# Moving one of ten per-head weight blocks into the plain stage, and the attention steps into the middle of blocks

## What is computed

```python
h = _rmsnorm(x, norm_g[l])
proj = jnp.einsum('bsd,df->bsf', h, w_in[l])
aq, ak, av, az = parts[0:4]            # branch A: 8 heads, differential attention
oa = _diff_attention(aq, ak, av, lam, slopes_a)
ya = rmsnorm(oa) * (1 - lam_init) * jax.nn.silu(az)
# branch B: three groups of q, k, v (dilations 1, 4, 16), mixed by their softmax sums
yb = ob.reshape(bsz, seq, B_WIDTH) * jax.nn.silu(bz)
# branch C: gated convolution of three taps
yc = cb * conv * jax.nn.silu(cz)
merged = sum over branches of gates[:, :, n] * (y_n @ w_branch_n)
x = x + merged @ w_out;  out = _rmsnorm(x, final_g)
```

## Time and profile before

| | |
|---|---|
| median of 3 runs | 2505.21 us (2503.38 to 2506.18) |
| the profiled execution | 2505.15 us, of which the traced span is 2503.4 us |
| PE busy | 2484.4 us, 99% of the span |
| DVE, ACT busy | 1945.7 us (78%), 1069.8 us (43%) |
| granted PE clock, mean | 0.999 of full speed |

### The profile page before, as it was taken

One profiled execution on the slowest core, in us unless ns is written; L12 is line 12 of the kernel. 1 busy time (PEld: TensorE's weight loads), 2 busy tenths in 40 slices (PEclk: granted clock), 3 DMA queues, 4 the chain that ended last, 5 costly groups with the idle time before them and its releaser, 6 DMA issues.

```text
span 2503.4 us, 30481 instructions
## 1 busy us (share of the span) xinstructions
PE 2484.4 (99%) x11454; PEld 2053.7 (82%) x11454; DVE 1945.7 (78%) x2266; ACT 1069.8 (43%) x1329; POOL 0.2 (0%) x4
## 2 busy tenths in 40 slices
PE   9999999999999999999999999999999999999998
PEld 8888888888888888888887788888878888788887
DVE  8797788566676767767678887788878888898875
ACT  5343333334333333333434433344444445655644
POOL 0000000000000000000000000000000000000000
PEclk9999999999999999999999999999999999999999
DMA  8255444686776667766535545445565456787666
GB/s 317 95 198 188 150 133 143 203 301 214 252 266 231 223 213 248 264 234 225 191 106 193 203 168 193 170 154 193 181 218 203 160 197 219 261 286 247 226 227 202
DMA packets 184902, 519.15 MB, mean 207 GB/s; under 512 B 14129, under 2 KB 59442, under 8 KB 181042
## 3 DMA queue, kind: packets, MB, share of 16 engines
q1 hardware_dynamic: 87872, 342.62, 39.9%
q10 hardware_dynamic: 96882, 174.55, 19.8%
HBM read 420.64 MB, written 96.47 MB: 207 GB/s over the span
## 4 chain that ended last, share of the span: by engine, by line
PE 92%; DVE 3%; DMA 3%; ACT 1%; issue 1%; DVEq 0%; ACTq 0%
PE proj L621 13%; PE proj L623 13%; PE proj L622 13%; PE sc_ps L621 6%; PE sc_ps L622 6%; PE sc_ps L623 6%; PE tr_ps L621 6%; PE tr_ps L622 6%; PE tr_ps L623 6%; PE o_ps L622 4%; PE o_ps L623 4%; PE o_ps L621 4%; PE tr_ps L664 1%; DVE w_lo L1547 1%; DMA rows<-c_dram 1%; DMA raw<-s_dram 1%
## 5 line engine op out<-in xcount | busy, mean ns | idle before, releaser
L1008 ACT ACTIVATE w_hi<-raw 128x1024 fp32r<-128x1024 f32 x296 | 314.0, 1061 | 430.3 <-PE proj L623 138.1
L1008 ACT ACTIVATE w_hi<-kb 128x1024 fp32r<-128x1024 f32 x280 | 297.2, 1062 | 442.6 <-PE proj L623 156.9
L1547 DVE TENSOR_TENSOR w_lo<-raw,w_hi 128x1024 fp32r<-128x1024 f32 x296 | 361.2, 1223 | 156.2 <-ACT w_hi L1008 155.3
L1547 DVE TENSOR_TENSOR w_lo<-kb,w_hi 128x1024 fp32r<-128x1024 f32 x280 | 342.7, 1224 | 116.6 <-ACT w_hi L1008 116.0
L621 PE MATMUL proj<-act_hi,w_hi 128*128 128x512 f32 x1024 | 405.8, 396 | 1.7 <-DVE w_lo L1591 1.7
L623 PE MATMUL proj<-act_hi,w_lo 128*128 128x512 f32 x1024 | 399.6, 390 | 0.0
L622 PE MATMUL proj<-act_lo,w_hi 128*128 128x512 f32 x1024 | 398.7, 389 | 0.0
L1057 ACT ACTIVATE w_hi<-raw 128x1024 fp32r<-128x1024 f32 x128 | 135.6, 1060 | 344.8 <-PE proj L623 339.9
L1591 DVE TENSOR_TENSOR w_lo<-raw,w_hi 128x1024 fp32r<-128x1024 f32 x128 | 156.6, 1224 | 103.1 <-ACT w_hi L1057 102.6
L623 PEld LDWEIGHTS proj<-act_hi,w_lo 128*128 128x128 f32 x1024 | 192.2, 188 | 41.3
L621 PEld LDWEIGHTS proj<-act_hi,w_hi 128*128 128x128 f32 x1024 | 192.8, 188 | 40.2 <-DVE w_lo L1591 1.9
(11 more groups left out here) (310 smaller groups left out, 4765.1 us busy)
## 6 DMA issues: line engine op xcount, KB each, us to landing
raw<-wg SPq DMA_DIRECT2D x128, 512.0 KB, 3.9
raw<-wst SPq DMA_DIRECT2D x128, 512.0 KB, 4.9
kb<-wg SPq DMA_DIRECT2D x28, 2048.0 KB, 7.6
ssum<-ws ACTq DMA_DIRECT2D x24, 2048.0 KB, 9.3
s_dram<-ssum ACTq DMA_DIRECT2D x24, 2048.0 KB, 7.7
raw<-s_dram SPq DMA_DIRECT2D x96, 512.0 KB, 4.4
raw<-ws SPq DMA_DIRECT2D x72, 512.0 KB, 4.1
kb<-wg SPq DMA_DIRECT2D x56, 512.0 KB, 6.3
```

The lines of the kernel that those rows point to most:

```text
L1008: nc.scalar.activation(w_hi[r % RING][:, :], src, ACT.Copy).then_inc(hi_done, 1)
L1547: tt(w_lo[r % RING][:, :], src, w_hi[r % RING][:, :].bitcast(f32), ALU.subtract).then_inc(lo_done, 1)
```

## The change

The numbering of the units changes: 9 entries and 14 units a head, and 7 quads before the branch C quads where there were 6. AZ is the plain group at the start, with weights as the stationary operand, so that the result is already transposed; it is stored to `z_dram`, comes back by head (`load_z`) and is scaled by DVE (`scale_z`). AV is quad 3. In the heads, steps stand between a block's two multiplications. (Of the diff, the parts that the steps below need.)

```diff
-NBLK1, NHU1 = 10, 16
+NBLK1, NHU1 = 9, 14
-QUADS_V, QUADS_C, QUADS_G, QUADS_O = 6, 10, 16, 2
+QUADS_V, QUADS_C, QUADS_G, QUADS_O = 7, 11, 17, 2
-SUMS_FIRST = (0, 4, 8, 12)
-SUMS_LOOP = (2, 6, 12, 16, 20, 24, 28, 34, 40, 44)
+SUMS_QUAD, SUM_QUAD_AT = 9, (13, 14, 15, 16)
+SUMS_FIRST = (0, 4, 8)
+SUMS_LOOP = (0, 4, 8, 12, 16, 20, 24, 28, 32, 36)
...
# plain_quad (PE)
-                            end = three(plain[half][b][:, :], act_hi[:, k, ts], act_lo[:, k, ts], w_hi[slot][:, cs], w_lo[slot][:, cs],
+                            end = three(plain[half][b][:, :], w_hi[slot][:, ws], w_lo[slot][:, ws], act_hi[:, k, :], act_lo[:, k, :],
...
# blocks (PE), between the two multiplications of a block
-                    if last and w == 9:
-                        values_a(i)
-                        probs_b(i, 0)
-                        scores_b(i, 1)
+                    if 4 <= w < 8:
+                        scores_a(i, w - 4)
+                    if w == BZ:
+                        scores_b(i, 0)
+                    if 5 <= w < 9:
+                        probs_a(i, w - 5)
+                    if w == 4 and not fresh:
+                        probs_b(i - 1, 3)
                     pe.wait_ge(lo_done, NHU1 * i + (R_H + t + 2))
                     multiply(h.bank(w), h.slot(t + 1), act_hi, act_lo, 8, False, True)
                     if w < 4 and not fresh:
                         scores_b(i - 1, w)
-                    if w < 5 and not fresh:
+                    if w < 4 and not fresh:
                         probs_b(i - 1, w - 1)
...
-                    if w == 5 and not fresh:
-                        values_b(i - 1)
-                    if 4 <= w < 8:
-                        scores_a(i, w - 4)
-                    if 5 <= w < 9:
-                        probs_a(i, w - 5)
-                    if w == 8:
-                        scores_b(i, 0)
...
+                    if w == 4 and not fresh:
+                        values_b(i - 1, o_ps, (o_free, 2 * i))
+                    if w == BZ:
+                        values_a(i)
+                        scores_b(i, 1)
+                        probs_b(i, 0)
...
# the first branch C quad (PE)
-                return {ON_X: [pb[2], pb[1]], ON_Z: sc_ps, ON_Y: pairs[2]}[CHAIN[p]]
+                return {ON_X: [pb[2], pb[1]], ON_Z: pairs[2], ON_Y: sc_ps}[CHAIN[p]]
-                            scores_b(HEADS - 1, 3)
+                        if n in (1, 3):
+                            scores_b(HEADS - 1, (n + 3) // 2)
-                            values_b(HEADS - 1)
+                            values_b(HEADS - 1, sc_ps[0], (biased, 8 * HEADS + 1))
...
# head (ACT)
+                    if 5 <= w < 9:
+                        turned_a(i, w - 5)
+                    if w == 4 and not fresh:
+                        turned_b(i - 1, 3)
+                    if 4 <= w < 8:
+                        exps_a(i, w - 4)
+                    if w == BZ:
+                        exps_b(i, 0)
                     split(t + 1)
...
+                        load_z(i)
...
-                    if w == AZ:
+                    if w == 7:
                         tanh_half(i, AZ)
...
# head (DVE)
+                    split(t)
...
+                    if 4 <= w < 8:
+                        bias_a(i, w - 4, fresh)
+                    if w == BZ:
+                        bias_b(i, 0)
                     if 5 <= w < 9:
-                        norm_a(i, w - 5)
-                    if w == 9:
-                        norm_b(i, 0)
-                    split(t)
+                        turned_a(i, w - 5)
+                    if w == 4 and not fresh:
+                        turned_b(i - 1, 3)
                     if w == Q0:
                         low_turn(h, AQ)
                     if w == K0:
                         low_turn(h, AK)
+                        if not fresh:
+                            inverse_a(i - 1)
+                            norm_o(i - 1)
                     if last:
                         combine_h(w)
                     if w == 4 and not fresh:
                         low_v(2 * i, v_b)
-                        inverse_a(i - 1)
-                        norm_o(i - 1)
...
-                    if w == 8:
+                    if w == BZ:
                         low_v(2 * i + 1, v_a)
-                    if w == 9:
                         silu(i, 0, AZ)
+                        norm_b(i, 0)
+                    if 4 <= w < 8:
+                        norm_a(i, w - 4)
                     scale_block(h, w)
+                    if w == 7:
+                        scale_z(i)
                     split(t + 1)
```

More of the change, by code:

```diff
@@ L702, in probs_b, with values_b @@
                 turn(i, TURN_P[c] + 1, [pr[:, n * P:(n + 1) * P] for n in range(4, 6)])
-            def values_b(i):
+            def values_b(i, bank, free):
                 pe.wait_ge(t_free, len(TURN_SPLIT) * i + (1 + len(TURN_SPLIT)))
@@ L855, in free_g @@
                     return tg_free, [len(TURN_COPY) * HEADS + 1] * 2
-                if CHAIN[p] == ON_X:
+                if q == QUADS_V + 1 and p == P5:
+                    back = (QUADS_V, 5)
+                elif CHAIN[p] == ON_X:
                     back = (q - 1, 5) if p == 0 else (q, {2: 0, 4: 2, 6: 4}[p])
@@ L1143, in squares_o @@
                 nc.scalar.activation(sq_hi[:, :], o_ps[:, :], ACT.Square).then_inc(sq_ready, 1)
+                if last:
+                    nc.scalar.activation(o_a[:, :], o_ps[:, :], ACT.Copy).then_inc(o_free, 1)
             def root_o(i, bank):
@@ L1177, in head @@
                         comb_high(6, t2[0], f2, (comb_sum, 6))
-                    if last and w == 9:
-                        squares_o(i)
-                        turned_b(i, 0)
+                    if 5 <= w < 9:
[6 more added lines that the diff above has]
+                        exps_b(i, 0)
                     split(t + 1)
@@ L1201, in head @@
                             load_v(i, Q_V + g, v_g[g], vg_in, True)
-                    if w < 5 and not fresh:
+                    if w < 4 and not fresh:
                         turned_b(i - 1, w - 1)
-                    if 5 <= w < 9:
-                        turned_a(i, w - 5)
-                    if w == 9 and not last:
+                    if w == BZ:
                         turned_b(i, 0)
@@ L1705, in scale_block, with scale_z, bias_a @@
                 ins.then_inc(evac_done, 1)
-            def bias_a(i, q):
+            def scale_z(i):
+                dve.wait_ge(za_in, 16 * i + 16)
+                tt(z_a[:, :], z_a[:, :], rstd[:, :], ALU.mult).then_inc(z_scaled, 1)
+            def bias_a(i, q, fresh):
                 n = P * (q + 1)
                 dve.wait_ge(s_ready, 8 * i + (q + 1))
-                if q:
+                if q or not fresh:
                     dve.wait_ge(p_ready, 8 * i + q)
-                else:
+                if q == 0:
                     dve.wait_ge(mask_a_in, 16 * i + 16)
@@ L1853, in head @@
                         bias_b(i - 1, w)
-                    if 4 <= w < 8:
-                        bias_a(i, w - 4)
-                    if w == 8:
-                        bias_b(i, 0)
-                    if w < 5 and not fresh:
+                    if w < 4 and not fresh:
                         turned_b(i - 1, w - 1)
-                    if 5 <= w < 9:
-                        turned_a(i, w - 5)
                     if w == 3:
@@ L2045, in _ @@
                         if n == 5:
+                            bias_b(HEADS - 1, 3)
                             turned_b(HEADS - 1, 2)
```

158 lines of the change are left out of this document (84 added, 74 removed).

## The result

The changed kernel takes 2560.38 us (median of 4, 2559.31 to 2561.66) where the kernel before takes 2504.3 us on the same chip: a ratio of 1.0224, 95% interval 1.0206 to 1.0242, or 56 us slower. The forecast was 2541, with a range up to 2560.

What follows compares the result with a forecast made beforehand. The prediction took TensorE (PE, busy 99%) to bound every stage. Waits of 46.9 us less 10.9 us for 48 fewer matmuls gave +36 us on 2505.2, so 2541, with a range of 2517 to 2560.

Steps and rivals of the forecast that it cites:

- Q1 of heads 1, 3, 4, 6: Block Q1: PE waits 5.1 us a head for `norm_b` and the bias, behind additions and reciprocal on DVE; 20 us.
- K2: Block BZ, heads 0, 1, 3, 4, 6: `scores_b(0)` waits for K2's `scale_block`, 0.9 us each, 4.5 in all.
- heads 2 and 5 together: Waits per head: 0.3 us for part 3 in Q1, 1.2 in Q0, 2 before `values_b`, 4 in BZ.
- head 7: `combine_h`, 2.3 us, stands in Q1: a wait of 2.6 us; another combination in BZ: 1.5 us.
- the quad: First branch C quad: part 3 one step later, reciprocal still before unit 7's low part; 1.9 us more (0 to 3).
- the last quad before the heads: Additions there make PE wait 1 us (0 to 3).
- 94 + 6: Expected length in us of a head of k = 1, where it was 105.
- no row here shows such a fall in the middle: Granted clock: rows showed a fall only near the end, so the waits were summed without any clock loss.
- rival 1: Heads: six waits (four in Q1, two in BZ) halve the clock, 2.5 us each, 15 us, 2556; chance 0.14.
- That queues absorb all (2): Faster: Q1's four waits vanish if the chain ends before PE's request, other waits under 1 us; 2496, chance 0.10.
- "About even" (3): Half of the Q1 waits and the smaller ones hidden, 11 us lost, 2505; chance 0.03.
- "removes nothing" (4): The count of matmuls stays, so the change does not remove what it says; chance 0.01.

Runs made afterwards that it cites:

- experiment 1: Changed kernel with spare matmuls put where PE waits in heads 1 to 7: 2544.54 us, 1.017.
- Experiment 5: Changed kernel with heads 1 to 6 written out instead of a loop, on PE, ACT and DVE: 2556.16 us, 1.0209.
- experiments 6: Changed kernel with branch B's part 3 put back by half a block in block Q1, ACT and DVE reordered to match: 2525.32 us, 1.0081.
- experiment 8: Changed kernel without the heads' additions (three one-column copies in their place, loads and stores kept): 2509.33 us, 1.0023.
- Experiments 7: Changed kernel with part 3 put back by half a block and, in BZ of heads 2 and 5, the additions behind `scale_block`: 2514.15 us, 1.0037.
- experiment 11: The order of experiment 7, with the first branch C quad's reciprocal six units later and heads 1 to 6 written out: 2506.13 us, 1.0007.
- experiment 10: The order of experiment 7, with Q0 and K2 additions behind `scale_block`, the quad's reciprocal six units later and the loop written out: 2555.14 us, 1.0202.

## Why the prediction was right and wrong

**The gain.** Right: 48 matmuls, 76.5 us for the new quad where 76.2 were worked out, 87.1 less in the heads.

**The waits.** Right in place, and nearly in sum: the terms were 46.9 us, what was measured of them, net of what was there before, is 40.2. Term by term, forecast against measured: Q1 of heads 1, 3, 4, 6 20.4 against 4 x 4.84 = 19.4; K2 4.5 against 5 x 0.43 = 2.1; heads 2 and 5 together 15 against 14.9 (`root_o` 1.2, part 3 0.6, `values_b` 3.7, `values_a` 9.3); head 7 2.6 and 1.5 against 2.5 and 0.15; the quad 1.9 against 0.95; the last quad before the heads 1 against 0.2. The large terms of Q1 and BZ came within 16%; the small ones (K2, `root_o`, the quad, BZ of head 7) were half of what was forecast, or less. A head of k = 1 took 102.2 us (AQ turned at 649.0 in head 1, at 751.2 in head 2) where "94 + 6" was forecast; its one fall of the clock took 2.1 of them.

**What failed** is the step "no row here shows such a fall in the middle", by which the sum took the clock at nothing and left it to rival 1, at 0.14 and 15 us. In its place stands a loss of 16 us by experiment 1, 19 us by the windows of the falls. The row for it was there, and the waits that I had forecast were as long as the stretch that ended in that fall. The two reasons against were both weak: the six small matmuls between the two waits in Q1 did not hold the clock up, and DVE's time to catch up was worth little, since the slow stretch reaches beyond the wait into full work. Rival 1 had the mechanism and nearly the size, with six falls of about 5 us where there were nine of 3.4 or 6.8; its 2556 came nearest to the 2560.4 measured.

**What was missing** is the jump of the loop: 4.90 us where 1.71 had been, 3.2 us. Experiment 5 shows that it goes when the loop is written out. Why it grew stays open: before, the profile puts it down to a low part, after to issue, and no run here separates the two.

With the estimated 3.9 us that the view of waits leaves out, 40.2 + 3.2 + 3.9 + 18.9 - 10.9 = 55.3 us, against 54.3 between the spans: each term is read or worked out by itself, and the sum closes within 1 us.

**The rivals.** That queues absorb all (2) fell: 28% of idle time on DVE did not help, because the chain's distance was the limit. Its condition was the right one though, the chain ending before PE's request: experiments 6 and 8 nearly meet it from either side and are at 2525 and 2509. "About even" (3) and "removes nothing" (4) fell with the first page.

**Left open.** Experiments 7 and 11 are some 4 us slower than their waits and falls account for (the eleventh: waits from 20 us on of 17.4 against 8.4, one fall worth 1.7, less 10.9, would make 2503.2 of span, and it is 2507.1). The trace places more than half of it: from 20 us on 28 waits are listed where the kernel before has 13, at 0.16 us each 2.4 us more. It shows head by head, from one turn of AQ to the next: 105.37 us in a head of the loop before, so 94.49 with two units less; with listed waits and falls taken off it is 94.7 to 95.2 us in experiment 11 and 94.5 to 94.6 in experiment 8, which has few waits. The rest, 1 to 2 us, is within what single executions differ by. Branch AV as a quad and AZ plain were not tried apart from the new order, so it is not shown that the new order was needed for them.

## What to carry to other kernels

When PE is the bound, a change that shortens a stage shortens the distance between every step and its use: redo the chain of each step in its new distance, and read which engine's queue a moved step now stands in front of, ACT's DMA issues and stores above all. Price a wait of PE of some 2 us or more above its length, for the clock that it may take down: in the changed kernel the shortest with a fall behind it was 1.87 us and the longest without one 2.63, and 43 us of added waits brought 16 to 19 us of clock with them. And where a wait follows from PE asking early, try putting the request back before touching the busy engine: half a block later was worth 35 us, three rearrangements of DVE's work between 10 and 14.

## What was not expected of the hardware

- The granted clock falls in the middle of a kernel after waits of 1.8 us (experiment 11; the row below has 1.87 in the changed kernel) to 7 us, also where six small matmuls split 4.84 us in 1.67 and 3.17. Not every such wait brings a fall: the same 1.87 us in head 2 had none, and the 2.63 us in the first branch C quad had one in experiment 1 and none in the changed kernel. The clock stayed at 0.50 for 3.4 or 6.8 us (10.2 once, in experiment 10), into full work. The row is the wait in head 5; the fall begins at 1105.5:

```profile
1105.03 1.22 PE L716 MATMUL o_ps<-pt_g,v_g 128*128 128x128 f32 x6 [1.87 <-DVE v_lo L1816]
```

- At the jump of the loop PE stood 1.7 us in one kernel (there the profile names a low part) and 4.5 to 5.4 in nine that have the changed heads, in some order; written out there was no wait there, but the kernel before became 4 us slower.
- In the changed kernel the issue of the mask load in K2 held ACT's queue for 5.11 and 4.19 us in heads 2 and 5, and the other twelve issues of mask loads 0.35 to 1.44. The issues of the two `v_g` loads took 1.30 us there in head 2 and 2.40 before the change.
